# Second layer's modulation multiplied at the experts' begins, and the first 22 rows of its first sparse tile beside the keys

## The reference

```python
for i in range(DEPTH):                       # 2 layers
    mod_l = split_cols(cond_lat @ w_mod[i] + b_mod[i], (D_MODEL,) * 6)
    ...
    h_lat = h_lat + mod_l[2] * o_lat
    f_lat = modulate(rmsnorm(h_lat, norm2_g[i]), mod_l[3], mod_l[4])
    h_lat = h_lat + mod_l[5] * peer_ffn(f_lat, ...)
# peer_ffn, per token: 8 heads, 2 x 128 keys, 16 best pairs a head -> 128 experts
top_s, top_i = lax.top_k(s, PEER_TOPK)
best_s, best_j = lax.top_k(cand_s, PEER_TOPK)
ue = jnp.take(u, idx, axis=0)
ve = jnp.take(v, idx, axis=0)
act = jax.nn.gelu(jnp.einsum('cd,chkd->chk', xc, ue))
return jnp.einsum('chk,chkd->cd', g * act, ve)
```

## Time and profile before

| | us |
|---|---|
| median of 3 runs (4769.7 to 4795.25) | 4771.01 |
| profiled execution, its own time | 4783.03 |
| its span, first to last instruction | 4781.4 |

### The profile page before, as it was taken

One profiled execution on the slowest core, in us unless ns is written; L12 is line 12 of the kernel. 1 busy time (PEld: TensorE's weight loads), 2 busy tenths in 40 slices (PEclk: granted clock), 3 DMA queues, 4 the chain that ended last, 5 costly groups with the idle time before them and its releaser, 6 DMA issues.

```text
span 4781.4 us, 53394 instructions
## 1 busy us (share of the span) xinstructions
PE 4179.8 (87%) x18407; PEld 2873.7 (60%) x18407; DVE 3339.1 (70%) x6731; ACT 1307.1 (27%) x2628; POOL 1767.5 (37%) x1652
## 2 busy tenths in 40 slices
PE   7999976694999899999999979886657779999997
PEld 3676664483676666666666645553443446666665
DVE  2466665568889677777777846775588767777776
ACT  3231311111666211111111123331214652222222
POOL 0012111022665455566565600000126655454452
PEclk8999978797999999999999989998778989999998
DMA  6966774713999999999999926888518999999995
GB/s 235 286 198 200 228 224 140 262 58 106 360 408 346 389 363 400 396 389 390 368 390 391 392 99 189 227 222 233 181 52 320 381 365 398 391 389 400 394 393 224
DMA packets 514579, 1408.04 MB, mean 294 GB/s; under 512 B 45693, under 2 KB 128893, under 8 KB 509471
## 3 DMA queue, kind: packets, MB, share of 16 engines
q1 hardware_dynamic: 330014, 733.73, 46.0%
q0 software_dynamic: 184320, 671.17, 36.2%
HBM read 1226.46 MB, written 178.26 MB: 294 GB/s over the span
## 4 chain that ended last, share of the span: by engine, by line
PE 65%; DVE 14%; DMA 10%; ACT 3%; POOL 3%; issue 3%; SPq 0%; DVEq 0%; ACTq 0%; POOLq 0%
PE ps L1840 20%; PE ps L1831 17%; DMA peer_arena<-in_peer_u 4%; PE ps L1804 3%; PE ps L1518 3%; DMA u_rows<-mixer_arena 3%; PE ps L746 3%; PE ps L1227 2%; PE ps L1232 2%; DMA expert_rows<-u_rows,peer_arena 2%; PE ps L321 2%; PE ps L749 2%; DVE expert_rows L2085 2%; PE ps L815 1%; DMA u_rows<-hidden 1%
## 5 line engine op out<-in xcount | busy, mean ns | idle before, releaser
L1787 POOL DMA_INDIRECT expert_rows<-u_rows,peer_arena x640 | 829.1, 1296 | 1052.5 <-DVE expert_rows L2085 821.8
L1831 PE MATMUL ps<-part_arena,peer_part_arena 128*128 128x384 f32 (+1 forms) x4096 | 1031.4, 334 | 37.7 <-DVE peer_part_arena L2128 25.4
L2085 DVE SCALAR_TENSOR_TENSOR expert_rows<-expert_rows,mixer_in 128x1024 f32<-128x1024 f32 x640 | 762.2, 1220 | 114.3 <-DMA expert_rows<-u_rows,peer_arena 112.0
L1794 POOL DMA_INDIRECT expert_rows<-in_peer_v,peer_arena x640 | 742.5, 1160 | 223.9 <-issue 186.5
L1831 PEld LDWEIGHTS ps<-part_arena,peer_part_arena 128*128 128x128 f32 x4096 | 699.7, 190 | 110.1 <-issue 99.0
L1840 PE MATMUL ps<-best,peer_arena 128*128 128x512 f32 x1540 | 685.3, 592 | 0.0
L1831 PE MATMUL ps<-mixer_in_parts,peer_part_arena 128*128 128x384 f32 (+1 forms) x2048 | 633.7, 309 | 0.0
L2110 DVE SCALAR_TENSOR_TENSOR peer_arena<-expert_rows,peer_arena 128x1024 f32<-128x1024 f32 x445 | 571.7, 1285 | 35.0 <-DVE peer_arena L2110 1.9
L1804 PE MATMUL ps<-expert_rows,peer_arena 128*128 128x512 f32 x768 | 387.8, 653 | 202.9 <-ACT peer_arena L1919 202.7
L1840 PEld LDWEIGHTS ps<-best,peer_arena 128*128 128x128 f32 x1540 | 285.1, 189 | 296.0 <-issue 296.0
L1571 POOL TENSOR_TENSOR part_arena<-peer_arena,part_arena 128x1024 fp32r<-128x1024 f32 x32 | 76.5, 2392 | 1007.1 <-ACT part_arena L1548 1007.1
(11 more groups left out here) (273 smaller groups left out, 6104.7 us busy)
## 6 DMA issues: line engine op xcount, KB each, us to landing
peer_arena<-in_peer_u SPq DMA_DIRECT2D x256, 512.0 KB, 12.1
best<-in_peer_v SPq DMA_DIRECT2D x154, 512.0 KB, 8.2
mixer_arena<-in_peer_u SPq DMA_DIRECT2D x272, 256.0 KB, 7.4
u_rows<-mixer_arena SPq DMA_DIRECT2D x136, 512.0 KB, 5.0
hidden<-in_peer_u SPq DMA_DIRECT2D x240, 256.0 KB, 6.2
u_rows<-hidden SPq DMA_DIRECT2D x120, 512.0 KB, 5.1
gates<-peer_arena SPq DMA_DIRECT2D x20, 2048.0 KB, 10.7
peer_arena<-in_peer_v SPq DMA_DIRECT2D x52, 512.0 KB, 7.6
```

What stands on the lines that cost most here:

```text
L1787: pool.indirect_dma_start(u_ring[:, k % U_SLOTS, :], None, u_table, bass.IndirectOffsetOnAxis(u_index[s][:, m:m + 1], 0)).then_inc(u_row_i ...
L1794: pool.indirect_dma_start(v_ring[:, k % V_SLOTS, :], None, v_table, bass.IndirectOffsetOnAxis(v_index[s][:, m:m + 1], 0)).then_inc(v_row_i ...
L1831: mm = pe.matmul(ps[:, 6, 0:dense_tok], left[j % len(left)][:, c, :], right[:, c, :], start=at == 0, stop=at == len(todo) - 1)
L2085: dve.scalar_tensor_tensor(out=rows, in0=rows, scalar=1.0, in1=B.x[:, :, rows_at + s * P:rows_at + s * P + P], op0=ALU.mult, op1=ALU.mult, ...
```

## The change

1. Layer 1's 48 modulation tiles are divided. 24 (the mixer's) are multiplied at the very begin of layer 0's `peer`, in six loads of 2 MB (`front`), ahead of everything else in PE's list. 16 (the second norm's) stay in the lots, one before every fourth lot. 8 (the experts' gate) are multiplied at the begin of layer 1's `peer`, in four loads of 1 MB, again ahead of everything else in PE's list.
2. In layer 1 the stage `keys_and_rows` takes the place of `product_keys`. Its steps are written out instead of looped. After step 3 DVE chooses the pairs of heads 0 and 1 of the first sparse tile; in steps 5 to 15 it multiplies one group of rows a step (22 rows). 26 U rows and 16 V rows are gathered, 8 groups get their shares, and PE adds 12 rows, two after each score from step 10 on. They use four early slots each.
3. Layer 1's `peer` goes on from there: V rows from 16, U rows from 26, `choose(0)` for heads 2 to 7 in one part, eight groups in the ahead part (now beside both choices), 29 instead of 42 groups beside the lots. In both layers ACT's `exp(1)` now stands behind the ahead groups.

The core of the diff (moved helpers, `search_pairs`, `decode_pairs` and `index_pairs`, read as before except that they take the heads they work on):

```diff
+EARLY = (Early(0, 0, 0, 0, 0, 0, 0), Early(2, 11, 8, 8, 6, 26, 16))   # heads groups gelus shares sums u_rows v_rows
+CHOSEN_BEHIND, EARLY_FROM = 3, 5
+U_EARLY, V_EARLY = 4, 4
-            keys = make(product_keys, layer, segs)
+            keys = make(keys_and_rows if EARLY[layer].heads else product_keys, layer, segs)
...
+def keys_and_rows(B, layer, segs):
...
+    def tensor(pe):
...
+        for j in range(STEPS):
+            if j + 1 < STEPS:
+                project(j + 1)
+            score(j)
+            if group_at(j) >= 5:
+                spread(group_at(j) - 5)
...
+    def gpsimd(pool):
...
+        for j in range(STEPS):
+            split_low(j)
+            if group_at(j) >= 1:
+                gather_u(group_at(j) - 1)
+            if group_at(j) >= 6:
+                gather_v(group_at(j) - 6)
+        for a in range(group_at(STEPS) - 1, E.u_rows // GROUP):
+            gather_u(a)
+            if a < 13:
+                gather_v(a - 5)
...
+        for j in range(STEPS):
+            strongest(j)
+            if j == CHOSEN_BEHIND:
+                choose()
+            if group_at(j) >= 0:
+                products(group_at(j))
+            if 0 <= group_at(j) - 2 < E.shares:
+                shares(group_at(j) - 2)
...
 def peer(B, layer, segs):
-    AHEAD = 6
+    E = EARLY[layer]
+    AHEAD_AT = (0, 3, 5, 8, 10, 13, 15, 18) if E.heads else (16, 18, 20, 22, 24, 25)
+    AHEAD, EXP_FIRST = len(AHEAD_AT), 3 if E.heads else 0
+    G0, K0, SUMMED = E.groups, GROUP * E.groups, GROUP * E.sums
-    MOD = 6 * C
-    mod = ModTiles(B, (ar, Arena(y_tok[1])), "mod", 6 * C, 1, ps[:, 5, 0:2 * MOD]) if layer == 0 else None
+    FRONT, MOD, FRONT_EACH = (3 * C, C)[layer], (2 * C, 0)[layer], (4, 2)[layer]
+    mod = ModTiles(B, (ar, Arena(y_tok[1])), "mod", 9 * C, 1, ps[:, 5, 2 * FRONT:2 * FRONT + 2 * MOD]) if MOD else None
+    front = ModTiles(B, (front_space, front_space), "front", (6 * C, 11 * C)[layer], FRONT_EACH, ps[:, 5, 0:2 * FRONT])
...
     def gpsimd(pool):
-        for k in range(steps):
+        for k in range(E.v_rows, steps):
...
-            if k >= U_SLOTS:
-                pool.wait_ge(score_ok, k - U_SLOTS + 1)
+            if k >= E.u_rows:
+                if k - U_SLOTS >= K0:
+                    pool.wait_ge(score_ok, k - U_SLOTS + 1 - K0)
...
-            if k >= V_SLOTS:
+            if k - V_SLOTS >= SUMMED:
                 if k - V_SLOTS < first_rows:
-                    pool.wait_ge(s0_mm, k - V_SLOTS + 1)
+                    pool.wait_ge(s0_mm, k - V_SLOTS + 1 - SUMMED)
...
     def tensor(pe):
-        for a in range(AHEAD - 1):
+        pe.sem_inc(front.used, 2)
+        for n in range(FRONT // FRONT_EACH):
+            front.multiply(pe, n, n % 2, n * FRONT_EACH)
+        for a in range(E.sums, G0 + AHEAD - 1):
             spread(a)
         turn(0)
...
-                if mod and at % 2 == 0 and at // 2 < MOD:
-                    mod.multiply(pe, at // 2, at // 2 % 2, at // 2)
+                if at % 4 == 0 and at // 4 < MOD:
+                    mod.multiply(pe, at // 4, at // 4 % 2, at // 4)
...
     def scalar(act):
-        exp(0)
-        for a in range(AHEAD):
-            if a == 3:
-                exp(1)
-            gelus(a)
-            if a:
-                diagonals(a - 1)
+        for n in range(AHEAD):
+            if n == EXP_FIRST:
+                exp(0)
+            gelus(G0 + n)
+            if G0 + n:
+                diagonals(G0 + n - 1)
+        exp(1)
...
     def vector(dve):
-        for piece, _ in enumerate(choose(1)):
-            if piece in (0, 2, 4, 6, 8, 9):
-                products(ahead)
+        for piece, _ in enumerate(itertools.chain(choose(0), choose(1))):
+            if piece in AHEAD_AT:
+                products(G0 + ahead)
```

More of the change, by code:

```diff
@@ L1 @@
+import collections
 import itertools
@@ new lines, in search_pairs @@
+def search_pairs(dve, chain, settle, here, best, best_j, cand):
+    heads = range(here.shape[1])
+    for to, a, b in pairs_that_may_win(here[:, :, 0, :], here[:, :, 1, :], cand[0]):
+        chain.inc(dve.tensor_tensor(to, a, b, ALU.add))
+    chain.wait(dve)
+    yield
+    settle(dve)
+    for h in heads:
+        chain.inc(dve.max(best[:, h, 0:8], cand[0][:, h, :]))
+    chain.wait(dve)
+    yield
+    settle(dve)
+    for h in heads:
+        chain.inc(dve.max_index(best_j[:, h, 0:8], best[:, h, 0:8], cand[0][:, h, :]))
+        chain.inc(dve.match_replace(cand[1][:, h, :], best[:, h, 0:8], cand[0][:, h, :], LOWEST))
+        if h % 4 == 3 or h == heads[-1]:
+            chain.wait(dve)
+            yield
+            settle(dve)
+    for h in heads:
+        chain.inc(dve.max(best[:, h, 8:16], cand[1][:, h, :]))
+    chain.wait(dve)
+    yield
+    settle(dve)
+    for h in heads:
+        chain.inc(dve.max_index(best_j[:, h, 8:16], best[:, h, 8:16], cand[1][:, h, :]))
+    chain.wait(dve)
+    yield
+    settle(dve)
@@ L1747, in sync @@
     def sync(sp):
-        sp.dma_start(iota, B.a["iota"]).then_inc(iota_in, 16)
+        if not E.heads:
+            sp.dma_start(iota, B.a["iota"]).then_inc(iota_in, 16)
+        for n in range(FRONT // FRONT_EACH):
+            front.load(sp, n, n % 2)
         if mod:
+            if E.v_rows:
+                sp.wait_ge(s0_mm, E.v_rows - SUMMED)
             for n in range(2):
@@ L1898, in exp @@
             act.wait_ge(shifted, n + 1)
-            x = gate(n).rearrange("p h k -> p (h k)")
+            x = gate(n) if n else gate(n)[:, late]
             act.activation(x, x, ACT.Exp).then_inc(exp_ok, 1)
@@ L2064, in choose @@
[L2064 to L2072 removed]
+        def choose(n):
+            heads = slice(0, HEADS) if n else late
+            count = heads.stop - heads.start
+            best, best_j = S.kept[n % 2][:, heads], S.kept_j[n % 2][:, heads]
+            yield from search_pairs(dve, chain, settle, top[:, ORDER[n], heads], best, best_j, [x[:, heads] for x in cand])
+            here = gate(n)[:, heads]
+            chain.done(dve, dve.tensor_tensor(here, best, best[:, :, 0:1].to_broadcast([P, count, TOPK]), ALU.subtract))
+            dve.sem_inc(shifted, 1)
+            parts = PARTS if n == 0 else 1
+            for part in range(parts):
+                some = slice(*(heads.start + count * (part + x) // parts for x in range(2)))
+                pairs = slice(some.start * TOPK, some.stop * TOPK)
+                yield from decode_pairs(dve, chain, S, top_key[:, ORDER[n], some], S.kept_j[n % 2], pairs, [x[:, some] for x in differ])
+                if ORDER[n] >= nd:
+                    index_pairs(dve, chain, S, layer, ORDER[n] - nd, pairs)
+                    dve.sem_inc(index_ok, 1)
+                    yield
```

458 lines of the change are left out of this document (329 added, 129 removed).

## The result

| | before | after |
|---|---|---|
| median of 10 runs each, us | 4775.07 (4769.7 to 4795.25) | 4808.07 (4803.58 to 4815.37) |
| profiled execution, its own time | 4783.03 | 4807.4 |
| its span | 4781.4 | 4805.5 |

The ratio is 1.0064, with a 95% interval from 1.0053 to 1.0075: slower by 0.6%. The forecast was 4780 us with a range of 4722 to 4812.

A forecast was written before the change was run, and what follows sets the result against it. Bounds were taken by stretch: PE first in layer 0's lots, DVE and transfers close; row transfers in layer 1's lots. Terms +43 - 38 + 36 + 39 - 70 = +10 gave 4793 us profiled, 12 lower for the median: 4780, range 4722 to 4812.

The forecast's parts named there:

- The fronts' price: Modulation tiles at the begin of both layers' `peer`: PE at the lower clock throughout, 3.3 us a tile.
- Rival B: Both fronts: they run at the upper clock, 1.85 us a tile; time 4734 us; chance 0.15.
- Layer 0, ahead: +43 us: Layer 0 before its lots: the front delays row 0 and U 9, DVE stands still 39 us; +43 us.
- Layer 0, lots: -38 us: Layer 0's lots: 32 of 48 tiles leave PE and the transfers, 363 us become 325; -38 us.
- Layer 1, keys: +36 us: Layer 1's keys stage: early choice, row groups, late scores and last issues, less the loop's turns; +36 us.
- Layer 1, ahead: +39 us: Layer 1 before its lots: the front delays U 26, DVE stands still 39 us; 71 us become 110; +39 us.
- Layer 1, lots: -70 us: Layer 1's lots: 29 instead of 42 groups and fewer gathered rows, 278.5 us become 208; -70 us.
- C: Both layers' lots: they take DVE's pace, 312 and 196 us, 25 us less; time 4755 us; chance 0.15.
- A: Whole kernel: the likeliest case, the five stretch terms summed, 4780 us, own range 4762 to 4798; chance 0.48.
- D: Layer 1's keys stage: lockstep with the gathers, steps 11 to 15 up to 14 us; time 4808 us; chance 0.22.

The follow-up runs named there:

- e5: The changed kernel with one added 128x512 matmul, its result unused, ahead of each front tile in both layers; 4867.59 us, ratio 1.0186 to the kernel before.
- e6: The changed kernel without the 16 tiles in layer 0's lots, the front's sums added in their place (wrong results); ratio 1.0049 to the kernel before.
- e4: The kernel before with layer 1's keys stage written out, no early choice or rows, and exp(1) behind the ahead groups; 4774.43 us, ratio 0.9984.
- e2: The changed kernel without layer 1's early rows (product_keys again), both fronts and 16 tiles in the lots kept; 4804.62 us, ratio 1.0041 to before.
- e9: The changed kernel without layer 0's front, 40 tiles in its lots; early rows and layer 1's front of 8 kept; 4797.42 us, ratio 1.0043 to before.

## Why the prediction was right, and where it was off

**The fronts' price: right.** 3.3 us a tile were predicted, 3.43 measured; row 0 near 1224, seen at 1227.8. The granted clock of 0.50 read from the earlier trace rows held through a front of 84 us. The first 2 MB were used 8.5 us after their issue, for 8.4, though the row that this was read from names ACT, not the transfer, as what PE waited for. Rival B didn't come: in the front and in e5 PE was busy all the time and the clock stayed at 0.50. B was what the Trainium skill's sentence in "TensorE: Matmul & The Clock Gate", section "Part 1: The HAM clock gate (the "warmup" mystery)", that activity releases the throttle, would give when read simply; these traces don't agree with it for such tiles.

**"Layer 0, ahead: +43 us": the total right, by two misses that cancel.** The stall was 35.3 us, not 39, and the 7.5 us of waits beside the front's loads that stand ahead of it were not in the prediction, which priced the loads for PE only. Together they are 4 us more than its 39; row 0 and U 9 too came 4 us later than it said. Two waits of the kernel before, for the iota and the turned choice, shrank by 4.1 us and made up for it. The rows behind U 9 cost 1.5 us for 2, and `exp(1)` 2.4 for 2.5.

**"Layer 0, lots: -38 us": the step that failed.** The prediction took the new end from one row over 363 us: DVE's 301 us as a floor, the transfers at 376 GB/s, 325 as something between. Measured: -21. The runs put in its place: the lots have a stretch of full DMA engines and one of full DVE, and most of a gain in either resource falls into its own stretch. Of the 21 us, 18 lie before the eighth write of gates, where 16 of the 32 tiles had stood; the 16 of the last 32 lots gave 3. Together the 32 gave 0.65 us each, against the 1.85 us of PE that each frees; the 16 that stayed were worth 0.4 us each (e6).

**"Layer 1, keys: +36 us": right in kind, 6 us short.** By term: the choice of two heads took 10.3 us (L1508 at 3485.68 to the next L1969 at 3496.00) for 10 predicted; the loop's turns 9.6 for 9 (e4); a late step 9.80 for 9.95. What was mis-sized is the end: +4 for POOL's last issues, where the stage ended 14.7 us after the last product's end at 3602.3 instead of 3.6 after DVE's last work, +11. 10.55 us of it are the wait for the meeting.

**"Layer 1, ahead: +39 us": right, 38.** DVE stood 41.3 us for U 26 and 1.6 for row 27, with 39 and 3 predicted; the 2.5 us for `exp(1)` are no wait of DVE there. That the prediction costed the front and the early rows together here was needed: e2 and e9 show that the front costs 0 alone and 32 with the rows.

**"Layer 1, lots: -70 us": -74,** 220.6 us where 294.7 - 70 would be 224.7. The bytes were worked out low: 100.8 MB less 50 rows of 0.52 MB are 74.6 MB, 206 us and not 203, which changes nothing in the 208 that was taken.

**The rivals.** C, DVE's pace in the lots, gave 13 and 12 us less than A, so 322 and 213 us in the stretches of the table. It falls in layer 0 (352.0); layer 1's 220.6 lies between A's 224.7 and C's. D, lockstep in the keys' stage, named the measured time (4808), but by coincidence: the straight code cost nothing (e4), and steps 11 to 13 took 9.80 us each where D had up to 14. V rows were late twice only, at the first two (PE waited 5.1 us) and the last two (2.8 us). So it was A, 28 us over its forecast. The terms make 14 of these (+17 in layer 0's lots, +6 in the keys, -4 in layer 1's lots, -4 in small ones). The other 14 are the step from the profiled execution to the median, and rounding: I took 12 us off, as for before's three runs; over ten runs before's execution lay 8 us above its median, and after's 1 us below its own. That the time stayed inside the range is in part due to the range's width: D's 4808 had set its upper end.
